# A last attention turn with the panels of the next projection placed inside it

## The reference

```python
def fox_attention(q, k, v, logf):          # 16 heads of 64, blocks of 128 queries
    F = jnp.cumsum(logf, axis=-1)
    ...
        s = jnp.einsum('bhqd,bhkd->bhqk', qi, k) * scale
        s = s + Fi[..., None] - F[:, :, None, :]
        s = jnp.where(kpos[None, :] <= qpos[:, None], s, -jnp.inf)
        p = jax.nn.softmax(s, axis=-1)
        return jnp.einsum('bhqk,bhkd->bhqd', p, v)
...
o_a = rmsnorm_2(o_a, g_gla) * jax.nn.silu(r_a)             # first attention, done earlier
o_b = fox_attention(q_b, k_b, v_b, logf)                   # second attention
merged = jax.nn.sigmoid(gate_a) * (o_a @ w_pa) + jax.nn.sigmoid(gate_b) * (o_b @ w_pb)
return merged @ w_out
```

## Time and profile before

| | us |
|---|---|
| median of 3 runs | 2550.78 |
| lowest and highest run | 2549.82, 2558.14 |
| the profiled execution, as timed | 2549.82 |
| its span, first to last instruction | 2548.0 |
| TensorE busy in it | 2390.1 |
| mean granted TensorE clock | 0.948 of 2.4 GHz |

### The profile page before, as it was taken

The page is one execution under the profiler, slowest core; times in us unless marked ns, Lnnn a source line. Parts: engine busy times, 40 slices in busy tenths (PEclk is TensorE's granted clock), DMA queues, the critical chain, the costliest instruction groups (busy, mean ns, idle before and its releaser), DMA issues.

```text
span 2548.0 us, 34251 instructions
## 1 busy us (share of the span) xinstructions
PE 2390.1 (94%) x10490; PEld 1924.1 (76%) x10490; DVE 959.5 (38%) x1696; ACT 932.3 (37%) x1628; POOL 1038.5 (41%) x796
## 2 busy tenths in 40 slices
PE   7999987989999989999979999998999997999997
PEld 6888866778888868888866777786666785788885
DVE  5699977335505222100132344435334223210012
ACT  4333374334422323323323533334333343443331
POOL 4455444444444434444453433332110244444443
PEclk9999988999999999999989999998987897999998
DMA  4334442438738323333322233332110331333331
GB/s 145 97 95 116 120 124 75 157 120 282 249 111 273 93 69 91 98 98 96 99 63 76 79 99 99 95 122 88 34 33 13 115 97 52 87 99 95 99 95 58
DMA packets 130412, 267.89 MB, mean 105 GB/s; under 512 B 14336, under 2 KB 14464, under 8 KB 129696
## 3 DMA queue, kind: packets, MB, share of 16 engines
q1 hardware_dynamic: 119520, 236.51, 31.1%
q10 hardware_dynamic: 10816, 30.38, 3.1%
HBM read 252.12 MB, written 14.68 MB: 105 GB/s over the span
## 4 chain that ended last, share of the span: by engine, by line
PE 70%; issue 17%; POOL 7%; DVE 4%; ACT 1%; POOLq 0%; DMA 0%; DVEq 0%; ACTq 0%
PE bank L840 21%; PE bank L842 21%; PE bank L841 21%; POOL wlo L367 6%; PE bank L1135 2%; PE bank L1163 2%; PE bank L1137 1%; PE bank L1149 1%; PE bank L946 1%; DVE G L1576 1%; DVE G L1586 1%; DVE tmp L1484 0%; PE bank L932 0%; POOL G L383 0%; DVE G L1483 0%
## 5 line engine op out<-in xcount | busy, mean ns | idle before, releaser
L367 POOL TENSOR_TENSOR wlo<-raw,whi 128x512 fp32r<-128x512 f32 x750 | 984.3, 1320 | 1401.2 <-ACT whi L439 1400.2
L840 PE MATMUL bank<-a_hi,whi 128*128 128x512 f32 x1992 | 796.5, 400 | 20.6 <-POOL wlo L367 8.5
L841 PE MATMUL bank<-a_hi,wlo 128*128 128x512 f32 x1992 | 783.4, 393 | 0.0
L842 PE MATMUL bank<-a_lo,whi 128*128 128x512 f32 x1992 | 783.4, 393 | 0.0
L439 ACT ACTIVATE whi<-raw 128x512 fp32r<-128x512 f32 x750 | 466.0, 627 | 756.4 <-PE bank L842 634.9
L840 PEld LDWEIGHTS bank<-a_hi,whi 128*128 128x128 f32 x1992 | 378.0, 190 | 122.6 <-issue 24.4
L842 PEld LDWEIGHTS bank<-a_lo,whi 128*128 128x128 f32 x1992 | 378.9, 190 | 81.0
L841 PEld LDWEIGHTS bank<-a_hi,wlo 128*128 128x128 f32 x1992 | 379.2, 190 | 75.4 <-issue 0.5
L840 PE MATMUL bank<-b_hi,whi 128*128 128x512 f32 x788 | 312.0, 396 | 24.5 <-DVE G L1498 8.5
L841 PE MATMUL bank<-b_hi,wlo 128*128 128x512 f32 x788 | 309.7, 393 | 0.0
L842 PE MATMUL bank<-b_lo,whi 128*128 128x512 f32 x788 | 309.6, 393 | 0.0
(11 more groups left out here) (232 smaller groups left out, 1932.9 us busy)
## 6 DMA issues: line engine op xcount, KB each, us to landing
raw<-d_stream SPq DMA_DIRECT2D x750, 256.0 KB, 2.6
G<-d_ada SPq DMA_DIRECT2D x72, 512.0 KB, 4.5
spill_rv<-tmp ACTq DMA_DIRECT2D x32, 256.0 KB, 2.1
G<-spill_rv ACTq DMA_DIRECT2D x4, 1024.0 KB, 9.2
G<-spill_rv ACTq DMA_DIRECT2D x2, 2048.0 KB, 9.4
G<-d_x ACTq DMA_DIRECT2D x4, 512.0 KB, 5.4
spill_ga<-G ACTq DMA_DIRECT2D x8, 256.0 KB, 3.6
spill_gb<-G ACTq DMA_DIRECT2D x8, 256.0 KB, 3.6
```

Of the source, the lines that this page charges most:

```text
L367: pool.tensor_tensor(wlo[:, s % SRING, :], raw[:, s % RING, :], whi[:, s % SRING, :].bitcast(F32), ALU.subtract).then_inc(lo_done, 1)
L840: pe.matmul(out_ps, w_hi, hi[:, k, :], start=first and q == 0, stop=False)
L841: pe.matmul(out_ps, w_lo, hi[:, k, :], start=False, stop=False)
L842: mm = pe.matmul(out_ps, w_hi, lo[:, k, :], start=False, stop=last and q == len(ks) - 1)
```

## The change

Four things move.

1. TensorE does one whole `pa` panel in 12 of the 16 steps of the last turn, in the steps with u % 4 of 0, 1 and 2. The four steps with u % 4 = 3 get none. The last four `pa` panels go between the groups of transposes of `OB`, one behind each second group. The stage of 16 panels in a row is gone. `pa` and `pb` have the same number of matmuls as before.
2. ACT does the splits of the stream that belong to them at the same places (12 in the last turn, 4 between its copies to `a_hi`). The gates are fetched by three DMAs, 2 MB and twice 1 MB; `GB2` is now four tiles where the queries and keys were (`QF`) and four where the probabilities were. All 16 sigmoids go in pairs into the stage of `pb`.
3. DVE cannot multiply `pa` by the gates yet, whose place is taken until the attention is over. It copies each finished tile out of PSUM (`keep_pa`: six in the last turn, two behind it), into seven free tiles and `sq`. The product with the gate follows from there, in the stage of `pb`, one more instruction for each tile.
4. DVE's loop has three turns, and the last one is written out, as on TensorE and ACT.

The line numbers of the new code are shifted: L840 to L842 are L851 to L853, L1149 is L1166, L1135 and L1137 are L1152 and L1154, L1163 is L1184, L1179 is L1198, L439 is L446, L774 and L783 are L781 and L790.

The whole diff:

```diff
--- before.py
+++ after.py
@@ -198,7 +198,14 @@
         PR, PT = tiles(B0, 2), tiles(B0 + 2 * T, 2)
 
         FHL, FLO, NFH, ONES_R = b_lo[:, 9, :], b_lo[32:48, 10, :], b_hi[:, 8:10, :], b_lo[:, 8, 0:P]
-        GA2, GB2 = tiles(12 * T, KD), tiles(B0, KD)
+        GA2, PA7 = tiles(12 * T, KD), tiles(B0 + 4 * T, 7)
+
+        def gb2(m):
+            return QF[:, m, :] if m < 4 else tiles(B0, 4)[:, m - 4, :]
+
+        def pa_out(m):
+            return PA7[:, m, :] if m < 7 else sq[:, 0, :]
+
         assert B0 + 11 * T <= G_END and 20 * T <= X0
 
 
@@ -783,6 +790,8 @@
                         act.activation(PT[:, w % 2, 0:n], bank[4 + w % 2][:, 0:n], ACT.Copy).then_inc(fox_pt, 1)
                     if next_qk and u < 16 and u % 2 == 0:
                         tick("qkb", i, 8 + u // 2, 1)
+                    if not next_qk and u < 16 and u % 4 < 3:
+                        tick("pa", 0, 3 * (u // 4) + u % 4, 1)
                     if next_qk and u in (9, 11):
 
                         keep_qk(i, 4 + u // 10)
@@ -797,21 +806,23 @@
 
             act.wait_ge(fox_o, 4 * FOX_HEADS + 2)
             act.dma_start(GA2[:, :, :], spill_rv[:, 2 * KD:3 * KD, :]).then_inc(ld_ga, 16)
-            act.dma_start(GB2[:, :, :], spill_rv[:, 3 * KD:4 * KD, :]).then_inc(ld_gb, 16)
+            act.dma_start(QF[:, :, :], spill_rv[:, 3 * KD:3 * KD + 4, :]).then_inc(ld_gb, 16)
+            act.dma_start(tiles(B0, 4), spill_rv[:, 3 * KD + 4:4 * KD, :]).then_inc(ld_gb, 16)
             for m in range(KD):
                 act.wait_ge(ob_t, m + 1)
                 act.activation(a_hi[:, m, :], bank[6 + m % 2][:, :], ACT.Copy).then_inc(a_hi_w, 1)
+                if m % 2:
+                    tick("pa", 0, 12 + m // 2, 1)
             act.wait_ge(ld_ga, 32)
-            for m in range(KD):
-                tick("pa", 0, 2 * m)
-                act.activation(GA2[:, m, :], GA2[:, m, :], ACT.Sigmoid).then_inc(gate2, 1)
-            act.wait_ge(ld_gb, 32)
-            for m in range(KD):
-                act.activation(GB2[:, m, :], GB2[:, m, :], ACT.Sigmoid).then_inc(gate2, 1)
-            for m in range(KD):
-                tick("pb", 0, 2 * m)
-                act.wait_ge(b_val, KD + m + 1)
-                act.activation(b_hi[:, m, :], tmp[:, m % 2, :], ACT.Copy).then_inc(b_hi_w, 1)
+            act.wait_ge(ld_gb, 48)
+            for m in range(KD + 1):
+                if m < KD:
+                    act.activation(GA2[:, m, :], GA2[:, m, :], ACT.Sigmoid).then_inc(gate2, 1)
+                    act.activation(gb2(m), gb2(m), ACT.Sigmoid).then_inc(gate2, 1)
+                    tick("pb", 0, 2 * m)
+                if m:
+                    act.wait_ge(b_val, KD + m)
+                    act.activation(b_hi[:, m - 1, :], tmp[:, (m - 1) % 2, :], ACT.Copy).then_inc(b_hi_w, 1)
             for m in range(KD):
                 tick("wout", 0, 2 * m)
                 wait_used(act, "wout", 0, 2 * m + 1)
@@ -1119,6 +1130,12 @@
                 mm.then_inc(oa_t, 1)
             pe.wait_ge(ld_v, 32)
 
+            def pa_panel(p):
+                if p % 2 == 0:
+                    bank_free("pa", 0, p // 2)
+                h = p % 2
+                panel("pa", 0, p, range(4 * h, 4 * h + 4), bank_of("pa", p // 2)[:, :], OPB, h == 0, h == 1)
+
             def fox_turn(i, next_qk):
                 def scores(u):
 
@@ -1158,6 +1175,10 @@
                         k = 2 * (u % 4)
                         panel("qkb", i, 8 + u // 2, (k, k + 1), bank_of("qkb", j)[:, :], OPA, u % 4 == 0, u % 4 == 3,
                               q0=k % 4, done=u % 2 == 1)
+                    elif u % 4 < 3:
+                        if u == 0:
+                            pe.wait_ge(opb, FILL_B["oa"] + KD)
+                        pa_panel(3 * (u // 4) + u % 4)
                     pe.wait_ge(fox_pt, i * 16 + (u + 3))
                     for j in range(t + 1):
                         mm = pe.matmul(bank[4 + u % 2][:, 0:FOX_HD], PT[:, u % 2, j * P:(j + 1) * P],
@@ -1173,12 +1194,11 @@
             for m in range(KD):
                 if m >= 2:
                     pe.wait_ge(opa, FILL_A["ob"] + m - 1)
-                else:
-                    pe.wait_ge(opb, FILL_B["oa"] + KD)
                 for t in range(4):
                     mm = pe.transpose(bank[6 + m % 2][:, t * P:(t + 1) * P], OB[:, t, m * P:(m + 1) * P], ident)
                 mm.then_inc(ob_t, 1)
-            stage8("pa", OPB, opb, FILL_B["oa"], 2)
+                if m % 2:
+                    pa_panel(12 + m // 2)
             stage8("pb", OPA, opa, FILL_A["ob"], 2)
             for m in range(KD):
                 tile8("wout", 0, m, OPB, opb, FILL_B["merged"], m == 0)
@@ -1725,8 +1745,13 @@
                     dve.tensor_tensor(b_lo[:, m - 1, :], tmp[:, (m - 1) % 2, :], b_hi[:, m - 1, :].bitcast(F32),
                                       ALU.subtract).then_inc(opb, 1)
 
+            def keep_pa(m):
+                wait_used(dve, "pa", 0, 2 * m + 1)
+                dve.tensor_copy(pa_out(m), bank_of("pa", m)[:, :]).then_inc(evac_of("pa", m), 1)
+
             dve.wait_ge(ld_f, 16)
-            with dve.Fori(0, FOX_HEADS // 4) as i:
+
+            def fox_turn(i, with_pa):
                 def forget_sums(h):
 
                     if h >= 2:
@@ -1744,7 +1769,6 @@
                     dve.tensor_scalar(small[:, 6, t:t + 1], small[:, 0, u % 2:u % 2 + 1], -1.0, None, ALU.mult)\
                        .then_inc(fox_m, 1)
 
-                own.begin(i, 16 * 3)
                 forget_sums(0)
                 maximum(0)
                 maximum(1)
@@ -1759,26 +1783,32 @@
                     dve.tensor_scalar(OB[:, t, ds(i * (4 * FOX_HD) + h * FOX_HD, FOX_HD)],
                                       bank[4 + u % 2][:, 0:FOX_HD], small[:, 1, u % 2:u % 2 + 1], None, ALU.mult)\
                        .then_inc(fox_out, 1)
-                own.end(FOX_HEADS // 4)
+                    if with_pa and u in (1, 4, 6, 9, 12, 14):
+                        keep_pa((1, 4, 6, 9, 12, 14).index(u))
+
+            with dve.Fori(0, FOX_HEADS // 4 - 1) as i:
+                own.begin(i, 16 * 3)
+                fox_turn(i, False)
+                own.end(FOX_HEADS // 4 - 1)
+            fox_turn(FOX_HEADS // 4 - 1, True)
             for m in range(KD):
                 dve.wait_ge(a_hi_w, FILL_A["ob"] + m + 1)
                 dve.tensor_tensor(a_lo[:, m, :], bank[6 + m % 2][:, :], a_hi[:, m, :].bitcast(F32), ALU.subtract)\
                    .then_inc(opa, 1)
-            for m in range(KD):
-                wait_used(dve, "pa", 0, 2 * m + 1)
-                dve.wait_ge(gate2, m + 1)
-                dve.tensor_tensor(GA2[:, m, :], bank_of("pa", m)[:, :], GA2[:, m, :], ALU.mult)\
-                   .then_inc(evac_of("pa", m), 1)
+                if m == 4:
+                    keep_pa(6)
+            keep_pa(7)
             for m in range(KD + 1):
                 if m < KD:
+                    dve.wait_ge(gate2, 2 * m + 2)
+                    wait_evac(dve, "pa", 0, m)
+                    own.next(dve.tensor_tensor(GA2[:, m, :], pa_out(m), GA2[:, m, :], ALU.mult))
                     wait_used(dve, "pb", 0, 2 * m + 1)
-                    dve.wait_ge(gate2, KD + m + 1)
 
                     dve.wait_ge(opb, FILL_B["merged"] + m - 1)
-                    dve.tensor_tensor(tmp[:, m % 2, :], bank_of("pb", m)[:, :], GB2[:, m, :], ALU.mult)\
+                    dve.tensor_tensor(tmp[:, m % 2, :], bank_of("pb", m)[:, :], gb2(m), ALU.mult)\
                        .then_inc(evac_of("pb", m), 1)
                     wait_evac(dve, "pb", 0, m)
-                    wait_evac(dve, "pa", 0, m)
                     dve.tensor_tensor(tmp[:, m % 2, :], tmp[:, m % 2, :], GA2[:, m, :], ALU.add).then_inc(b_val, 1)
                 if m:
                     dve.wait_ge(b_hi_w, FILL_B["merged"] + m)
```

## The result

| | us |
|---|---|
| changed kernel, median of 4 runs | 2523.37 (2518.61 to 2526.74) |
| kernel before, median of 4 runs beside it | 2551.51 (2549.82 to 2558.14) |
| ratio | 0.9888, 95% interval 0.9874 to 0.9901 |
| the profiled execution after, as timed | 2526.05 |

The change makes the kernel 28 us faster, 1.1%. The forecast was 24 less (2526.7), in a range of 2520 to 2538. The two profiled executions differ by 23.8 us (2549.82 to 2526.05).

The account below looks back on a forecast made before the run. TensorE bounds this part at whichever clock it is granted, 0.54 in the last turn. Last turn 71.1, falls 3 and transposes with panels 15.6 make 89.7 us for 113.8, 24.1 less: 2526.7 us, range 2520 to 2538.

Parts of the forecast that it names:

- 68.6 at the high clock: Last turn with no low clock: attention work 31.2 us, twelve panels 34.1, idle at start 1.9, waits at end 1.4.
- 2.5 for the start: Start of the last turn: clock low for 5 us, half of it lost; bounds 1.6 and 8.5 us.
- 3 in all for falls: Clock drops to half in four panel-free places, chance one in three each, 2.5 us apiece; bounds 0 and 13.4.
- The fourth place: Steps 14 and 15, their two waits and the first two transpose groups: some 6 us where the clock may drop.
- the group of transposes at the high clock: One of eight groups of four OB transposes, taken as about 0.53 us; 4.2 us for all, 15.6 with four panels.
- Cost zero: In pb, DVE's extra product per tile, 0.69 us, would not delay TensorE, which sets the pace at 43.6 us.
- the reserve that I named: DVE's idle time in pb, 3.42 us for each tile, with room for the extra product.
- A: Clock never drops in the last turn's panel-free steps: 3 us less than forecast, 2523 to 2524; chance 0.22.
- B: Clock drops at all four panel-free places: 10.4 us more, 2537, or 2543 with a long low start; chance 0.11.
- C: In the last turn the attention's chain through ACT becomes the bound: 10 us more, 2537; chance 0.06.
- D: High clock never returns in the last turn: 42 us slower than before, 2593; chance 0.03.
- E: Panels wait in the last turn for a late bank or wlo: time as before, within 0.3%; chance 0.04.

Follow-up runs that it names:

- the pair of fillers: Kernel before plus 144 unused matmuls, spread over 12 steps of the last turn (2562.05 us, ratio 1.0039) or in a row ahead of it (2583.01 us, 1.0121).
- the second profile: The changed kernel timed and profiled once more, nothing altered; median 2520.73 us, ratio 0.989 to the kernel before, profiled execution 2518.64 us.
- the seven profiles named above: Two of the changed kernel, five of variants with the same panel-free or filler-free last-turn steps; ratios to the kernel before from 0.9858 to 1.0039.
- s2_between_only: Changed kernel with its twelve last-turn panels in a row behind that turn, four still between the transposes; 2546.38 us, ratio 0.9983 to the kernel before.
- r4_copies_only: Changed kernel with all 16 pa panels back in a row behind the transposes, all else kept; 2553.58 us, ratio 1.0006 to the kernel before.
- s4_whole_qkb: Changed kernel with query and key panels of the first three turns done whole in even steps; 2522.53 us, ratio 0.9892 to the kernel before.
- u1_first_even: Changed kernel with early dense work ahead of each turn's first scores and last-turn panels spread evenly over 16 steps; 2516.28 us, ratio 0.9859 to the kernel before.

## Why the prediction was right

**The bound.** It was named rightly as the granted clock, and the pair of fillers shows it without moving any useful work: 144 matmuls for 10 us in the turn, 31 in front of it.

**The last turn.** Forecast 68.6 at the high clock and 2.5 for the start, 71.1, and 3 in all for falls. Measured 72.1 with one fall behind the start (the other came behind the turn's end), and 70.5 in the second profile with none. A head took 16.46 for 16.3. The start was low for 3.4 us in both profiles, near the lower bound of 3.2; I took 5. The price of 2.84 us a panel, switch included, held (1944.54 to 1947.39: 2.85).

**The falls.** One in three for each of four places gave 1.3; 2 and 0 were seen, and 7 in the 28 places of the seven profiles named above. The prediction put them in steps 3, 7, 11 and at the end, and all 7 were in these places. The fall at step 11 came with no idle row ahead of it, so a full TensorE did not keep the clock on thin work, as the last turn of before had shown (58.6 of 61.3 us busy at 0.50). The fourth place was 4.4 us long (2001.86 to 2006.30), not some 6. The Trainium skill, TensorE: Matmul & The Clock Gate, "Why this matters for your kernels", names idle gaps between bursts of matmuls as what makes the clock fall. By that rule there would have been no fall at step 11; the trace shows one.

**The transposes.** Forecast 15.6, measured 16.1 with a fall and 14.6 and 14.5 without (second profile, `s2_between_only`). The mis-sized term is the group of transposes at the high clock, taken as 0.53 us. That was worked out from the row's own 1.97 us, which is longer than the step to the next row (and half of it over 1.91 is 0.52). Two groups with a panel behind them step on after 0.80 us, 0.40 a group: 3.2 us for eight instead of 4.2. The panels there took 2.82. This 1.1 us too much hid part of the falls.

**DVE in `pb`.** Cost zero was right for TensorE, the sum behind it was not. I took 0.69 us for every operation. The addition took 1.83:

```profile
2038.17 0.69 DVE L1809 TENSOR_TENSOR tmp<-bank,G 128x512 f32<-128x512 f32 x1 [1.69 <-PE bank L853]
...
2038.88 1.29 POOL L374 TENSOR_TENSOR wlo<-raw,whi 128x512 fp32r<-128x512 f32 x1 [1.24 <-ACT whi L446]
2038.89 1.83 DVE L1812 TENSOR_TENSOR tmp<-tmp,G 128x512 f32<-128x512 f32 x1
```

DVE's idle time for each tile fell from 3.42 to 1.69 us: 0.69 for the new product and 1.1 for this. TensorE did not wait, and the copies and the new placement alone cost nothing that the medians tell (`r4_copies_only`), but half of the reserve that I named is used up.

**The size.** The profiled pair gave 23.8 us for a forecast of 24.1; the medians gave 28. That the pair is so near is in part luck: the profiled execution of before was its fastest run, the one of after among its slowest, and in it a stretch that gained 25.6 instead of 24.1 met 1.3 us lost ahead of the turn and 0.5 behind `pb`. The forecast was built on one execution, and the changed kernel varies from 2518.6 to 2528.0 over both rounds with the falls and low starts that a run happens to get.

**Rivals.** A (nothing falls) was seen in one profile of the two, and its 2523 to 2524 is nearer to the median of 2523.4 than the forecast is; the medians can't choose between them. B, C, D and E were not: TensorE had no idle row released by ACT in a step with a panel, and no low stretch in the turn was longer than 3.4 us. In two variants the start of the last turn was low for 10.2 us (`s4_whole_qkb`, `u1_first_even`), which is part of what B allowed for.

## What to carry to other kernels

Read the granted clock beside TensorE's busy time: the stretch here that was 94% busy at 0.54 had room for dense matmuls at a third of their price, and unused matmuls put there and put elsewhere measure that room before anything is rearranged. Spread the dense work so that no long piece of small matmuls stands alone: three steps in a row lost the clock, single ones cost nothing that the medians could tell. Put some between transposes that wait for one another, where it covers the waits. Then put dense work that waits for nothing in front of each pipeline that has to fill.

## What the runs showed of the hardware

- Attention matmuls over 64 or 32 rows or into 64 columns, and transposes of 128x128, kept TensorE 96% busy (56.16 of 58.30 us) and left it at 1.2 GHz for a whole turn. 36 matmuls of 128x512 in each head raised that to a mean of 0.95 (turn of 72.1 us), 12 in each head to 0.69 (66.1 us).
- The clock falls or not at the same place of the same program from one execution to the next: 0 or 2 times in the turn's thin places in two profiles of the changed kernel. All four falls inside the turn in seven profiles began within 0.4 us of the end of a step without a panel. What decides whether one comes stays open; no run here was made to tell.
- A DVE addition with both inputs in SBUF that starts 0.01 us after a GpSimd instruction takes 1.83 us instead of 0.69; the last one of the stage, with no GpSimd instruction beside it, took 0.69 again. 1.83 is the 1.29 us of the GpSimd instruction and 0.54 more. The product with one input in PSUM took 0.69 throughout. The Trainium skill, SBUF — State Buffer, "SBUF: two separate sides", says that such a DVE operation and GpSimd take a shared pair of ports in turn, each for its whole instruction. The trace agrees, with these 1.83, 1.29 and 0.69 us; no run was made to part it from other causes.
